# Scaling attention probabilities on ScalarE instead of VectorE in a two-layer decoder step

## What is computed

```
qg = q.reshape(b, tq, NSA_KV, NSA_REP, HEAD_DIM)
p2 = jax.nn.softmax(s2.reshape(*s2.shape[:4], -1), axis=-1)      # branch 1, selected blocks
o_slc = jnp.einsum('btgrnj,btgnjd->btgrd', p2.astype(vg.dtype), vg)
p = jax.nn.softmax(jnp.where(m, s, NEG), axis=-1)                # branch 2, window
o = jnp.einsum('btgrs,bsgd->btgrd', p.astype(v.dtype), v)
o_nsa = jnp.sum(o_nsa3 * pr['n_g'][..., None].astype(o_nsa3.dtype), axis=-2)
```

## Time and profile before

| | us |
|---|---|
| median of three runs | 2053.99 |
| their range | 2051.23 to 2055.41 |
| the profiled execution | 2060.65 |
| its span, first to last instruction | 2058.9 |
| busy in it: TensorE | 1840.3 (89%) |
| VectorE | 969.6 (47%) |
| ScalarE | 459.7 (22%) |
| GpSimd | 535.5 (26%) |

### The profile page before, as it was taken

How to read it: one execution, slowest core, us unless ns; L and a number is a source line. 1 busy time by engine, 2 the same in 40 slices (tenths; PEclk the granted TensorE clock), 3 DMA queues, 4 the chain that set the end, 5 groups by cost and what they waited for, 6 DMA issues and landing times. The chain is left out here.

```text
span 2058.9 us, 25458 instructions
## 1 busy us (share of the span) xinstructions
PE 1840.3 (89%) x9456; PEld 1467.6 (71%) x9456; DVE 969.6 (47%) x1812; ACT 459.7 (22%) x1187; POOL 535.5 (26%) x718
## 2 busy tenths in 40 slices
PE   6999987668798999999989998885688999999998
PEld 5888764335477888888878886643444888888887
DVE  4025326986455434343320552379764544344433
ACT  2112232222322211111111223231323222111202
POOL 0007002754222221212300240056360322222223
PEclk8999988778789999999999998787785999999999
DMA  6411312444611222222241204045283112222223
GB/s 209 153 42 42 104 21 105 163 164 166 203 42 65 99 82 82 82 82 82 82 169 58 82 1 124 2 144 204 82 286 83 55 68 82 82 93 101 94 82 124
DMA packets 107931, 210.35 MB, mean 102 GB/s; under 512 B 28128, under 2 KB 37136, under 8 KB 103328
## 3 DMA queue, kind: packets, MB, share of 16 engines
q1 hardware_dynamic: 92944, 141.58, 20.7%
q0 software_dynamic: 13824, 67.12, 9.0%
q10 hardware_dynamic: 1040, 0.00, 0.0%
HBM read 200.00 MB, written 17.06 MB: 105 GB/s over the span
## 5 line engine op out<-in xcount | busy, mean ns | idle before, releaser
L524 PE MATMUL ps<-xt,ring 128*128 128x260 f32 x1536 | 353.0, 389 | 11.0 <-DVE xt L650 11.0
L524 PEld LDWEIGHTS ps<-xt,ring 128*128 128x128 f32 x1536 | 294.0, 194 | 57.7 <-issue 12.1
L1199 PE MATMUL ps<-cst,xt 128*128 128x128 f32 x328 | 76.3, 349 | 73.1 <-DVE xt L1314 62.0
L1199 PEld LDWEIGHTS ps<-cst,xt 128*128 128x128 f32 x328 | 44.8, 175 | 114.9 <-DVE xt L1314 81.8
L2091 ACT ACTIVATE tt<-ps 128x260 f32<-128x260 f32 x108 | 41.8, 387 | 356.0 <-PE ps L1990 236.2
L2091 ACT ACTIVATE scr<-ps 128x260 f32<-128x260 f32 x108 | 41.8, 387 | 351.5 <-PE ps L1990 226.8
L1252 ACT ACTIVATE xt<-ps,small 128x512 f32<-128x512 f32 (+3 forms) x128 | 67.7, 529 | 216.4 <-DVE small L1330 216.4
L1798 POOL TENSOR_TENSOR tt<-ring,tt 128x1024 f32<-128x1024 f32 x32 | 82.6, 2594 | 65.0 <-DVE scr L1601 51.3
L596 ACT ACTIVATE tt<-ps 128x520 f32<-128x520 f32 x48 | 29.0, 604 | 312.6 <-PE ps L524 312.6
L1314 DVE TENSOR_SCALAR xt<-xt,small,gates 128x512 f32<-128x512 f32 (+3 forms) x128 | 96.8, 797 | 2.3
L671 DVE TENSOR_TENSOR big<-big 128x512 f32<-128x512 f32 (+1 forms) x10 | 6.9, 690 | 183.3 <-ACT big L583 183.1
(11 more groups left out here) (411 smaller groups left out, 3750.9 us busy)
## 6 DMA issues: line engine op xcount, KB each, us to landing
ring<-in_w_up SPq DMA_DIRECT2D x16, 2048.0 KB, 8.4
ring<-in_w_down SPq DMA_DIRECT2D x16, 2048.0 KB, 7.8
ring<-in_w_in SPq DMA_DIRECT2D x15, 2048.0 KB, 8.1
ring<-in_state_win_k SPq DMA_DIRECT2D x2, 2048.0 KB, 8.5
ring<-in_state_win_v SPq DMA_DIRECT2D x2, 2048.0 KB, 14.9
ring<-in_w_out SPq DMA_DIRECT2D x4, 1024.0 KB, 13.3
ring<-in_w_out SPq DMA_DIRECT2D x8, 512.0 KB, 16.7
out_s_win_k<-in_state_win_k SPq DMA_DIRECT2D x2, 2044.0 KB
```

The costliest lines, as they stand in the source:

```text
L524: ins = pe.matmul(self.ps[:, 2 * (u % 2) + half, 0:H], w[:, k, f * P:(f + 1) * P], self.xtv[:, k, half * H:(half + 1) * H], start=(k == 0) ...
L1199: ins = pe.transpose(turn_bank(g)[:, b * P:(b + 1) * P], prob[slot(w, g)][:, b * P:(b + 1) * P], self.c("ident"))
```

## The change

The probabilities are no longer scaled by VectorE. `norm` still makes the reciprocals, and then multiplies them by the gates of the two heads, a TENSOR_TENSOR of 128x2 with both inputs in SBUF (`w_ready`). A new function `scale` on ScalarE multiplies the two heads' probabilities by that weight, one ACTIVATE each with a scale per row, in place. It stands ahead of exp(u,0) of the next unit. The `yield` in ScalarE's steps moves ahead of copy(u-1,0), so that a sampled step now comes before that copy. Branch 0 keeps its scaling on VectorE and signals by `w_ready`. `turns` names the order of the query tiles, which stays as it was.

```diff
+        turns = (3, 2, 1, 0)
+        pairs = [(qt, br, r) for qt in turns for br in range(3) for r in ((None,) if br == 0 else range(4))]
+        n_heads = lambda w: 2 * sum(br > 0 for _, br, _ in pairs[:w])
...
-            pe.wait_ge(normed, 2 * w + (2 if br == 0 else g + 1))
+            if br == 0:
+                pe.wait_ge(w_ready, w + 1)
+            else:
+                pe.wait_ge(normed, n_heads(w) + g + 1)
...
+            def scale(w, g):
+                qt, br, r = pairs[w]
+                if br == 0:
+                    return
+                k = slot(w, g)
+                pr = prob[k][:, 0:(qt + 1) * P]
+                act.wait_ge(w_ready, w + 1)
+                act.activation(pr, pr, ACT.Copy, scale=rcp[:, k:k + 1]).then_inc(normed, 1)
...
             for u in range(U + 3):
+                if 1 <= u <= U:
+                    scale(u - 1, 0)
+                    scale(u - 1, 1)
                 if u < U:
                     exp(u, 0)
+                yield
                 if 1 <= u <= U:
                     copy(u - 1, 0)
-                yield
                 if u < U:
                     exp(u, 1)
...
-                k, nk = slot(w, 0), (qt + 1) * P
+                k = slot(w, 0)
+                gate = own_gates[:, qt, :, br].rearrange("p (g r) -> p r g", g=2)[:, r]
                 link(dve.reciprocal(rcp[:, k:k + 2], rsum[:, k:k + 2]))
-                for g in range(2):
-                    pr = prob[k + g][:, 0:nk]
-                    dve.tensor_scalar(pr, pr, rcp[:, k + g:k + g + 1], own_gates[:, qt, 4 * g + r, br:br + 1], ALU.mult,
-                                      ALU.mult).then_inc(normed, 1)
+                dve.tensor_tensor(rcp[:, k:k + 2], rcp[:, k:k + 2], gate, ALU.mult).then_inc(w_ready, 1)
```

More of the change, by code:

```diff
@@ L1142, in prompt_sparse @@
         pj = self.proj
-        qk_done, nmax_ready, exp_done, normed, turned, copied = (
-            self.sem(s) for s in ("ns_qk", "ns_negmax", "ns_exp", "ns_normed", "ns_turned", "ns_copied"))
+        qk_done, nmax_ready, exp_done, w_ready, normed, turned, copied = (
+            self.sem(s) for s in ("ns_qk", "ns_negmax", "ns_exp", "ns_weight", "ns_normed", "ns_turned", "ns_copied"))
         pv_done, o_read = self.sem("ns_pv"), self.sem("ns_o_read")
@@ L1154, in prompt_sparse @@
         own_gates = self.gates[:].rearrange("p t (h c) -> p t h c", c=3)
-        pairs = [(qt, br, r) for qt in (3, 2, 1, 0) for br in range(3) for r in ((None,) if br == 0 else range(4))]
+        turns = (3, 2, 1, 0)
+        pairs = [(qt, br, r) for qt in turns for br in range(3) for r in ((None,) if br == 0 else range(4))]
         U = len(pairs)
@@ L1209, in values @@
             if br == 0:
-                if qt < 3:
-                    pe.wait_ge(o_read, 3 - qt)
+                if turns.index(qt) >= 1:
+                    pe.wait_ge(o_read, turns.index(qt))
                 for q in range(4):
@@ L1289, in act_steps @@
                     qt = pairs[u - 3][0]
-                    act.wait_ge(pv_done, 5 * (4 - qt))
+                    act.wait_ge(pv_done, 5 * (turns.index(qt) + 1))
                     act.activation(self.xtv[:, 4:8, cols(qt)], self.ps[:, 5, :].rearrange("p (r q) -> p r q", r=4), ACT.Copy
@@ L1307, in norm @@
                     link(dve.tensor_tensor(wgt, wgt, own_gates[:, qt, :, 0], ALU.mult))
-                    dve.tensor_tensor(pv, pv, wgt.unsqueeze(2).broadcast_to([P, 8, 16]), ALU.mult).then_inc(normed, 2)
+                    dve.tensor_tensor(pv, pv, wgt.unsqueeze(2).broadcast_to([P, 8, 16]), ALU.mult).then_inc(w_ready, 1)
                     return
-                k, nk = slot(w, 0), (qt + 1) * P
+                k = slot(w, 0)
+                gate = own_gates[:, qt, :, br].rearrange("p (g r) -> p r g", g=2)[:, r]
                 link(dve.reciprocal(rcp[:, k:k + 2], rsum[:, k:k + 2]))
-                for g in range(2):
-                    pr = prob[k + g][:, 0:nk]
-                    dve.tensor_scalar(pr, pr, rcp[:, k + g:k + g + 1], own_gates[:, qt, 4 * g + r, br:br + 1], ALU.mult,
-                                      ALU.mult).then_inc(normed, 1)
+                dve.tensor_tensor(rcp[:, k:k + 2], rcp[:, k:k + 2], gate, ALU.mult).then_inc(w_ready, 1)
             def largest(u):
```

## The result

The changed kernel took 2026.4 us, the median of four runs (2020.6 to 2036.8), against 2054.7 (2051.2 to 2059.2) for the kernel before in the same comparison: a ratio of 0.9863, with a 95% interval of 0.9823 to 0.9902. A second comparison gave 0.9845 (0.9797 to 0.9893). The profiled execution took 2036.84 (span 2035.1), 23.8 us less than the profiled one of before.

A forecast was written before the change was run, and what follows sets the result against it. The prediction took the sparse attention stage to be bound by chains, no engine being full. Its terms, 3.0 - 13.2 - 1.0 + 0.5 = -10.7 us, gave 2043.3 us on the median's scale, with an 8-in-10 range of 2032.5 to 2054.

The forecast's parts named there:

- Held units of the cached keys, +3.0: Cached keys: three units a layer, where GpSimd's product holds VectorE, each 0.5 us later; +3.0 us over two layers.
- The held L1307 ended at 499.80, 0.03 after the product that held it; ... +0.5: Path to the transposes where GpSimd holds VectorE: they follow the product's end by 0.84 us instead of 0.35, +0.5.
- The sign that I had named for the forecast: Held cached-key units: the copy of keys should wait about 0.9 us for TensorE instead of 0.41.
- Rival A: Cached keys: the weight slips past GpSimd's product too, in two held units a layer; -9.6 us, total 2033.7; chance 17%.
- Softmax chain, -13.2: Sampled softmax chain: the weight passes the memset, so L1483 starts earlier; -6.8 and -6.4 us by layer, -13.2 in sum.
- This part moves as a block with its start: Values, then last query tile: the DMA-bound part moves with its first gather, expected near 482 instead of 487.31.
- Second L1314 gone, -1.0: Second layer's pair at 1351.87: half of its 2.2 us excess goes with the second scaling instruction; -1.0 us.
- the last tile, +0.5: Last query tile: scalings lie under the scores, only the very last unit is exposed; +0.25 a layer, +0.5 us.
- Nothing for the new order and for ScalarE's pair: ScalarE: sampled work ahead of copy(u-1,0) costs nothing; the two scalings ahead of exp(u,0) are hidden by VectorE work.
- The likeliest case at 50%: Whole kernel: the forecast itself, -10.7 us, to 2043.3 us, 0.52% less; chance 50%.

The follow-up runs named there:

- the kernel with units 0 to 11: The changed kernel with ScalarE's scaling only in units 0 to 11 (cached keys), the others scaled on VectorE as before; ratio 0.9863, -28 us.
- the ten-unit kernel: The changed kernel with ScalarE scaling only in units 4, 6, 8, 10 and 12 of each layer, 10 of 64; ratio 0.9866.
- the wide weight: The changed kernel with the weight written as a TENSOR_TENSOR of 128x128 from two broadcast inputs instead of 128x2; ratio 0.9853.
- unit 12 alone: The changed kernel with ScalarE scaling only in unit 12 of each layer, the other 31 units as before; ratio 0.9998.
- units 12 to 17 together: The changed kernel with ScalarE's scaling only in units 12 to 17, the sampled softmax chain; ratio 0.9908, -19 us.
- the two kernels for it: The changed kernel with no unit's scaling moved, only ScalarE's new order (1.0012), and with scaling moved only from unit 18 on (0.9997).
- the version with both edits: The changed kernel with the loads of the output weights held until the last cached values have landed; ratio 0.9795, median 2011.4 us.
- the third extra profile of before: The last of three more profiles of the unedited kernel before, nothing changed; that execution took 2063.3 us.

## Why the prediction was wrong, step by step

**Held units of the cached keys, +3.0: wrong, in sign and size.** It is the step "The held L1307 ended at 499.80, 0.03 after the product that held it; ... +0.5". I took it that what held L1314 and L1307 would hold the weight. The trace shows it held in none of the four units a layer, and the part gained 7.4 to 11.2 a layer. Against +3.0 the two profiled executions have -15.2 and -21.9 for both layers, a difference of 18 and 25, as large as the whole miss of 17 to 21. The sign that I had named for the forecast, the copy of keys waiting 0.9 for TensorE, didn't come: it waits 0.62 at 359.83 and 1.55 at 380.46, because VectorE now gets there early; the kernel with units 0 to 11 shows that this part alone is worth as much as the whole change, and the ten-unit kernel that the held units are enough. Rival A had the mechanism (-2.4 in a unit against the forecast, -1.9 against before; measured 2.0 at 377), but for two of four units and with a reason, the short duration, that the wide weight shows not to be needed. The row that spoke for it was there, in the timeline of before: L1619, 128x1024 with two inputs, starts 0.16 ahead of the product at 386.49 and takes its 1.21 us, while the product lasts 3.28 instead of 2.36.

```profile
386.33 1.21 DVE L1619 TENSOR_TENSOR scr<-ring,pos_k 128x1024 f32<-128x1024 f32 x1
```

It won; I had read only those that lost. That the direction of the forecast came out was partly luck: it rested on the chain alone, and had the part that paid most on the other side.

**Softmax chain, -13.2: the mechanism right, what reaches the end open.** The weight passes the memset in 0.16, and unit 13 gains 6.4 to 7.0 us on unit 12 in each layer of the eight profiled executions in which ScalarE scales unit 12. Not every one of them tests the memset, though: in the execution of 2021.5 us the weights of unit 12 started 2.15 ahead of it in both layers. From unit 12 to 17 the change kept -3.7 to -9.3 a layer, in sum -15.8 in one execution and -10.2 in the other, around the forecast. But unit 12 alone moved the measured time by -0.4 +- 4.9, and units 12 to 17 together by -19 +- 4.

**"This part moves as a block with its start": wrong.** In the execution of 2036.8 us the first gather of the first layer came 16.6 us earlier and the last product over values 15.4, but the stage ended only 11.2 earlier; in the other execution it was 17.7. What the forecast had left out is the loads of the output weights, which delay the last gather's landing, and TensorE's clock behind it, 0.50 or 0.93.

**Second L1314 gone, -1.0, and the last tile, +0.5: not told apart.** Between the stages -1.8 and -3.0 went away, among other differences of that size. In the last tile the units keep their 2.51 and 2.73 us, and the maxima still wait for TensorE, as forecast (timeline of the changed kernel, to be held against the earlier trace rows):

```profile
553.44 0.49 DVE L1346 TENSOR_REDUCE small<-ps 128x1 f32<-128x128 f32 x2 [0.81 <-PE ps L1190]
```

**Nothing for the new order and for ScalarE's pair: right**, 1.0012 and 0.9997 by the two kernels for it.

The likeliest case at 50% was thus wrong in its first term. A measurement of four runs had an interval of +-0.4%, not the 0.2% that I gave it. And a range whose lower end was rival A for two units a layer could not hold what four do.

## What to carry to other kernels

When two engines collide, list who won and who lost with head start and operand form, before pricing a new instruction at that place: one winner in the timeline (L1619) would have told more than the losers that I had read. Shift work only where its engine stands and someone waits for it, here four or five units in 32 a layer. And when a part is bound by DMA, price what follows in its queues: the next stage's loads, issued 6 us later, gave another 0.5%, and the version with both edits, at 0.9795, is the fastest here.

## What the runs showed of the hardware

Who got ahead when VectorE started an instruction shortly before a product of GpSimd (TENSOR_TENSOR, 128x1024, 2.36 us alone), all from the timelines of these kernels:

| VectorE's instruction | ahead by | taken (alone) | product |
|---|---|---|---|
| TENSOR_TENSOR 128x2, two inputs in SBUF | 0.04 to 0.12 | 0.16 (0.16) | 2.34 to 2.37 |
| the same, 128x128 (wide weight) | 0.04; 0.20 behind a gather | 0.29 (0.29) | 2.48; 2.37 |
| the same, 128x512 | 0.26 and 0.32 | 0.69 (0.69) | 2.65; 2.58 |
| the same, 128x512 | 0.02 behind a gather | 2.93 | 2.35 |
| the same, 128x1024 (L1619) | 0.16 | 1.21 (1.21) | 3.28 |
| TENSOR_SCALAR 128x512, scalars per row (L1314) | 0.01 to 0.08; 0.20 to 0.23 behind a gather | 2.64 to 2.71; 2.86 (0.54) | 2.34; 2.36 |
| the same | 0.09 to 0.54, not behind a gather | 0.54 | 2.67 to 2.35 |
| SCALAR_TENSOR_TENSOR 128x512 | 0.04; 0.20 behind a gather | 2.93; 3.12 (0.75) | 2.34; 2.36 |
| the same | 0.11 and 0.57, not behind a gather | 0.75 | 2.85; 2.40 |
| TENSOR_SCALAR 128x1 | any, also behind it | 0.20 (0.20) | 2.36 |

"Behind a gather" means that the product was queued behind a gather's DMA_INDIRECT and started 0.01 to 0.02 after it; before the other products GpSimd had stood idle for 0.3 us or more. A few hundredths of a microsecond decide over 2.4, and they are not the same for each form. For L1314 before a product that is not queued the edge lies between 0.08 (2.71 us, at 339.70 in the third extra profile of before) and 0.09 (0.54 us, at 337.92 in the first). The plain TENSOR_TENSOR won with 0.04. Behind a gather 0.20 was not enough for the forms with scalars per row, and was enough for the wide weight. The Trainium skill ("SBUF — State Buffer", section "Who interferes with whom") has an exclusive lock on the shared pair of ports, which goes to whichever instruction issues first, and lets `tensor_scalar` contend in its modes with two ports and `tensor_tensor` only through its second input. The trace agrees on who can contend: a memset holds a TENSOR_SCALAR of 128x384 (3.86 to 5.17 us instead of 0.48) and neither TENSOR_TENSOR (0.56) nor SCALAR_TENSOR_TENSOR (0.62), and a TENSOR_SCALAR of one column took 0.20 or 0.21 in each of the 12 cases inside a product. On "first" it differs, as far as recorded starts show the issue: by them L1314 was 0.01 to 0.23 first and lost.

Two cases stay open. A TENSOR_TENSOR that starts while another instruction of GpSimd runs, with a product queued behind it, can lose with more ahead: 0.31 in the memset shown above, and in the changed kernel L1326 of 128x128 lost with 0.53 and took 3.05, as it started 0.42 into a gather's DMA_INDIRECT. The weights that started 0.7 or more into one did not. And L1307 of 128x8 lost with 0.09, and with 0.06 to 0.13 in the other profiles, where a weight of 128x2 won with 0.04; the product was queued behind a DMA_INDIRECT in the one and waited for a semaphore in the other, which may be the reason, but no run here varied it alone.
